# Expert weights of a two-layer mixture-of-experts model: which loads are requested while the tokens are still being routed

## The reference

```
def run_block(args):
    xb, e = args
    return (jax.nn.silu(xb @ w1[e]) * (xb @ w3[e])) @ w2[e]
...
p_sel, g_idx = lax.top_k(p_group, 1)
p_top, e_local = lax.top_k(jax.nn.softmax(e_logits, axis=-1), TOP_K)
e_idx = g_idx * EXPERTS_PER_GROUP + e_local
```

## Time and profile before

| | |
|---|---|
| median of 3 runs | 2667.68 us (2663.33, 2667.68, 2667.91) |
| profiled execution: its own time | 2663.74 us |
| its span (first to last instruction) | 2661.5 us |
| mean granted clock of TensorE | 0.906 of full speed |
| PE busy | 2262.7 us, 85% of the span |
| DVE, ACT, POOL busy | 731.6, 605.4, 174.1 us |
| moved by DMA | 595.85 MB, mean 224 GB/s |
| of it on SP's queue | 515.42 MB |
| routing of layer 0 ends, experts' block begins | at about 886.8 us |
| routing of layer 1 ends, experts' block begins | at about 2045.3 us |

### The profile page before, as it was taken

How to read it: one execution, slowest core, us unless ns; L and a number is a source line. 1 busy time by engine, 2 the same in 40 slices (tenths; PEclk the granted TensorE clock), 3 DMA queues, 4 the chain that set the end, 5 groups by cost and what they waited for, 6 DMA issues and landing times. The chain is left out here.

```text
span 2661.5 us, 34953 instructions
## 1 busy us (share of the span) xinstructions
PE 2262.7 (85%) x15232; PEld 1083.6 (41%) x15232; DVE 731.6 (27%) x1142; ACT 605.4 (23%) x915; POOL 174.1 (7%) x126
## 2 busy tenths in 40 slices
PE   6598998987995599999999639995985999988874
PEld 3277886554453133333333224442433333322223
DVE  0522324653006111111111273544225111111104
ACT  2521113551005111111111144445013111111102
POOL 0001000000000000000000212223000000000002
PEclk8599999997997799999999759997896999999986
DMA  9600105206422789889999430001005899999985
GB/s 376 224 24 21 35 24 211 113 1 189 158 95 74 320 325 415 355 350 411 416 414 414 138 114 24 24 0 58 6 3 243 335 411 417 414 416 419 427 342 194
DMA packets 139501, 595.85 MB, mean 224 GB/s; under 512 B 25333, under 2 KB 52689, under 8 KB 114641
## 3 DMA queue, kind: packets, MB, share of 16 engines
q1 hardware_dynamic: 109232, 515.42, 48.7%
q0 software_dynamic: 11952, 43.52, 4.5%
q10 hardware_dynamic: 18160, 34.61, 3.6%
HBM read 534.79 MB, written 58.72 MB: 223 GB/s over the span
## 5 line engine op out<-in xcount | busy, mean ns | idle before, releaser
L1584 PE MATMUL ph<-w,x_t 128*32 128x512 f32 x6016 | 683.2, 607 | 40.2 <-DMA w<-in_exp_w 38.0
L1584 PEld LDWEIGHTS ph<-w,x_t 128*32 128x32 f32 x6016 | 190.7, 112 | 455.2 <-issue 427.8
L1597 PE MATMUL py<-w,g_t 128*32 128x512 f32 x3008 | 341.2, 594 | 1.0 <-DVE g_t L1703 1.0
L1697 DVE TENSOR_TENSOR hidden<-hidden,ph 64x512 f32<-64x512 f32 x94 | 102.1, 1086 | 779.1 <-ACT hidden L1655 779.1
L1167 PE MATMUL z<-Y,w_o 128*128 128x512 f32 (+1 forms) x640 | 256.2, 557 | 0.0
L1655 ACT ACTIVATE hidden<-ph 64x512 f32<-64x512 f32 x94 | 55.6, 592 | 697.9 <-PE ph L1584 697.9
L1889 PE MATMUL z<-hT,w_cd 128*128 128x512 f32 (+1 forms) x448 | 185.7, 572 | 7.5 <-ACT hT L478 4.9
L1597 PEld LDWEIGHTS py<-w,g_t 128*32 128x32 f32 x3008 | 93.8, 110 | 204.9 <-issue 203.6
L692 PE MATMUL z<-h_high,w_hi 128*128 128x512 f32 (+1 forms) x432 | 161.7, 374 | 15.4 <-DVE h_low L526 15.4
L1167 PEld LDWEIGHTS z<-Y,w_o 128*128 128x128 f32 x640 | 120.7, 192 | 129.2 <-issue 125.9
L1562 POOL DMA_INDIRECT x_rows<-h_tokens,index x47 | 44.4, 945 | 1807.7 <-PE px L1569 995.2
(11 more groups left out here) (293 smaller groups left out, 2102.8 us busy)
## 6 DMA issues: line engine op xcount, KB each, us to landing
w<-in_exp_w SPq DMA_DIRECT2D x192, 2048.0 KB, 15.2
ada_raw<-in_ada_w SPq DMA_DIRECT2D x24, 2048.0 KB, 8.7
y_slots<-y_rows ACTq DMA_DIRECT2D x188, 128.0 KB, 8.7
y_slots<-zero SPq DMA_DIRECT2D x29, 512.0 KB
h_tokens<-h_rows ACTq DMA_DIRECT2D x18, 512.0 KB, 2.9
w_ab<-in_w_in_ab SPq DMA_DIRECT2D x14, 512.0 KB, 3.9
w_cd<-in_w_in_cd SPq DMA_DIRECT2D x12, 512.0 KB, 6.4
x_t_saved<-xT SPq DMA_DIRECT2D x8, 640.0 KB, 8.1
```

The source lines that it names most:

```text
L1584: ins = pe.matmul(ph[row:row + UNIT, :], xt[:, k, at:at + UNIT], w13[place[2 * b + n] % RING][:, half, k, :], start=(k == 0), stop=(k == K ...
L1597: ins = pe.matmul(py[b % 2][row:row + UNIT, :], gt[:, k, n * UNIT:(n + 1) * UNIT], w2[place[2 * b + n] % RING][:, k, half * 512:(half + 1) ...
L1697: dve.tensor_tensor(hid[PAIR:P, :].rearrange("s (k q) -> s q k", k=FT), hid[0:PAIR, :].rearrange("s (q k) -> s q k", k=FT), ph[PAIR:P, :]. ...
```

## The change

In `route`, SP now issues only the up and gate weights (w1 and w3) of expert 0. The loads of expert 0's w2 and of expert 1's w1 and w3 are taken out there. In `experts`, SP first waits for `s_x` to reach 16, which is the landing of the first gather of token rows. Behind it SP issues expert 0's w2, and then experts 1 and 2 in full. All other waits, buffers and the order of the loads among themselves stay.

```
@@ -1287,8 +1287,6 @@
                 sp.wait_ge(s_table, 1)
                 first = self.expert_of(sp, 0)
                 self.load_up(sp, layer, ring, 0, first)
-                self.load_down(sp, layer, ring, 0, first)
-                self.load_up(sp, layer, ring, 1, self.expert_of(sp, 1))
                 for i in range(HROWS):
                     sp.wait_ge(s_hw[i], 16 * len(range(i, nt, HROWS)))
 
@@ -1528,8 +1526,9 @@
 
             @block.sync
             def _(sp):
-                self.load_down(sp, layer, ring, 1, self.expert_of(sp, 1))
-                for j in range(2, NE):
+                sp.wait_ge(s_x, 16)
+                self.load_down(sp, layer, ring, 0, self.expert_of(sp, 0))
+                for j in range(1, NE):
                     e = self.expert_of(sp, j)
                     if j >= RING:
                         sp.wait_ge(s_a, last[j - RING] // 2 + 1)
```

## The result

| | before | changed |
|---|---|---|
| median | 2667.80 us (4 runs, 2663.33 to 2668.73) | 2646.31 us (4 runs, 2642.22 to 2651.92) |
| profiled execution, its own time | 2663.74 us | 2651.92 us |
| its span | 2661.5 us | 2649.4 us |

The ratio is 0.9924, with a 95% interval of 0.9901 to 0.9947: 20.3 us less, between 14.1 and 26.4. The two medians alone lie 21.5 us apart. The forecast was 2644.5 us. The profiled execution of the changed kernel is the slowest of its four, so I compare stages, each counted from its own start.

The account below looks back on a forecast made before the run. It took TensorE to bound layer 0's experts and the weights' stream layer 1's. Gains of 9.9 + 6.5 us in layer 0 and 6.5 in layer 1, 22.9 together, led to a 2644.5 us forecast, range 2636 to 2655.

Parts of the forecast that it names:

- The end of routing in layer 0: Layer 0's first gather starts earlier because the stores of rows land sooner with fewer loads beside them; gain 9.9 us.
- The landing of the gather: First gather of each layer lands in 4.5 us with no new loads beside it; gain 6.5 and 6.8 us.
- The weights behind the wait: Counted from the gather's landing L, block 3's weights land at L + 35.8, before up(3) needs them; 0 us lost.
- the bound of -1.5 us: Layer 0, up(3): at 396 GB/s the weights land at L + 38.1, 1.5 us late.
- the slack of 3.4 us: Layer 1, up(3): time left between the landing of the weights at L + 35.8 and their need at L + 39.2.
- Layer 1: Layer 1's experts: the weights' stream can gain 7.3 us and TensorE's start gains 6.8; 6.5 us taken.
- The gather's 11 us are its own: Rival, first gathers: the landing stays slow; layer 0 gains 9.9 us, layer 1 0.5 or less; about 2657.5 us; chance 0.08.
- The weights are just late: Rival, both layers: stream at 396 GB/s, and up 0's tail beside the gather; gain 16.4 us, 2651.3 us; chance 0.14.
- The clock: Rival, TensorE's first products: clock after idle time shifts either layer by up to 2.5 us; chance 0.10 for over 2 us.
- TensorE waits at block 3: Rival, up(3): below 275 GB/s, waiting for experts 1 and 2 eats layer 0's 16.4 us; 2684 us at 250; chance 0.02.
- The signs: Expected trace: layer 0's gather starts about 877, stores' wait about 12 us, block 3's wait under 2, layer 1's about 38.0.

Follow-up runs that it names:

- e5: The changed kernel with expert 0's w1 and w3 issued behind SP's wait for the stores of rows, in both layers; 2646.70 us, ratio 0.9926.
- e1: The changed kernel without its new wait: the loads taken out of routing are issued at the start of the experts' block; 2660.98 us, ratio 0.9986.
- e7_best: The changed kernel with expert 0's w1/w3 behind the stores' wait in layer 0 alone, and experts 1 and 2's w1/w3 before their w2; 2645.59 us, ratio 0.9924.
- e4_ups_first: The changed kernel with w1 and w3 of experts 1 and 2 issued ahead of their w2, behind expert 0's w2; 2645.75 us, ratio 0.9924.

## Why the prediction was right

**The forecast as a whole** held: 2646.31 us against 2644.5, inside 2636 to 2655. The sum was 22.9 us; by the stages it is 19.3. By the ratio of the runs it is 20.3 us, with an interval (14.1 to 26.4) wide enough for both. That the median came within 2 us of the forecast is in part luck: the four executions spread over 9.7 us, and the forecast of the stages was 3.6 us too high. These are its steps.

**The end of routing in layer 0** is the term that was mis-sized: 9.9 us forecast, 6.9 measured (T to gather 11.46 to 4.55). The mechanism was right, as e5 and e1 show: the stores hold up the meeting of the engines, and the loads beside them are what slows them. Wrong was the working. I let 5.76 MB pass at 396 to 426 GB/s, added 1 us for the last landing, and had the stores landed 11.8 us behind the last one's issue. It took 14.5. In these rows the first stretch begins where my sum began (861.0 us, here 1.84 later) and ends with the landing:

```profile
862.84:880.54 17.70, 4.67 (x176) 3.71 (x174) 11.54 (x32) 3.84 (x8) 0.00 (x0) 0.65 0.89 342
...
870.00:874.00 4.00, 0.16 (x12) 0.16 (x16) 3.79 (x8) 0.00 (x0) 0.00 (x0) 0.50 1.04 442
874.00:877.50 3.50, 2.61 (x161) 2.26 (x157) 1.20 (x7) 0.00 (x0) 0.00 (x0) 0.50 0.95 370
877.50:880.60 3.10, 0.00 (x0) 0.00 (x0) 0.00 (x0) 0.00 (x0) 0.00 (x0) 0.50 0.33 131
```

342 GB/s over 17.7 us are 6.05 MB and not 5.76: more than three stores were still under way. That is worth 0.7 us at the rates of my sum. The 1 us for the last landing stood on no row. From 878.5 us on only 0.01 MB still moved, and the last landing came at 880.5, 2.0 us later. The remaining 1.0 us is the rate, 386 GB/s on the mean until 878.5. The gather then starts 1.2 us behind the landing, where I had taken 0.9.

**The landing of the gather** was forecast at 4.5 us in both layers and is 4.47 and 4.51 (4.61 and 4.38 again): 6.6 and 6.8 us gained against 6.5 and 6.8. By the rule of the Trainium skill's "DMA: Bandwidth & Descriptors", section "Anatomy of one DMA — SWDGE (gpsimd) path", it would have been 3.2 us, an estimate; in all twelve profiles, with 47 gathers each, none lands in less than 4.2 us.

**The weights behind the wait.** SP issued down 0 0.72 us behind the landing in both layers (0.76 forecast). Up(3) of layer 0 needed expert 2 at L + 36.6 exactly as worked out, but it was there at L + 37.6 instead of L + 35.8, so the bound of -1.5 us was the better guess: 1.03 us lost. The rate of the bound is the one that came, 399 GB/s from 887 to 912.5 us where I had taken 426. In layer 1 the slack of 3.4 us covered it. In the second profile of the changed kernel the clock was lower (0.81 from up(0) to up(2), against 0.94 in the first), up(3) stood 36.70 us behind up(0), and there was no wait.

**Layer 1** gained 6.81 us by the stages (6.69 in the second pair), 6.5 forecast. The shift of the start came through to the end unshortened, though the weights' stream sets the end there. The reason given, that the stream's idle time shrinks by about as much as the start moves, agrees with what the DMA engines moved in the 312.95 us from the issue of up 0 on, before and then changed:

```profile
2031.14:2344.09 312.95, 286.94 (x2681) 94.67 (x2685) 47.26 (x84) 45.48 (x67) 13.27 (x14) 0.95 0.97 398
...
2025.62:2338.57 312.95, 290.39 (x2709) 96.00 (x2713) 48.22 (x85) 46.06 (x68) 13.23 (x14) 0.96 0.99 407
```

9 GB/s more over 313 us are 2.8 MB, or 6.6 us at 426 GB/s, and in the first 113 us alone (365 and 389 GB/s) it is already 6.4 us. I had 7.3 us for the stream and took 6.5. With the 2 to 3 us by which layer 1 differs between profiles anyway, an agreement to 0.3 us is more than the forecast can claim.

**The rivals.** *The gather's 11 us are its own*: fallen, by 4.5 us with nothing beside it and 11.8 in e1. *The weights are just late*: its first half happened at less than half of its price (1.03 us of 2.5, all of it in layer 0), its second half (the tail of up 0 beside the gather) did not, but e5 shows what it costs, 6.78 us. *The clock*: it moves the first products by what I said, but the two profiles compared hardly differ in it (36.33 against 36.06 us in layer 1; in layer 0 the difference is the wait). Up(0) to up(3) takes 33.4 to 34.5 us in some stages and 36.0 to 36.7 in others. The same changed kernel had 34.53 and 36.70 in layer 0, so the spread is that of executions. This rival is worth as much as the smaller terms of the sum. *TensorE waits at block 3*: the wait is there, 1.03 us and not 16. The engines moved 399 GB/s from 887 to 912.5 us and 425 behind it, far from 275.

**The signs.** The landing (4.5 us), down 0 (0.72 us), block 3 (under 2 us) and the waits of layer 1 (37.0 us from 2100 us on) were as said. SP's wait for the stores was not: 17.2 us, where I had about 12. So the first gather of layer 0 started at 881.7 and not at 877, of which 1.84 us are this profile's lateness.

## What to carry to other kernels

A small gather that starts a stage should not share the DMA engines with prefetches that nobody needs yet; here 0.52 MB took 4.5 us alone and 9 to 12 us beside 2.10 MB or more asked for at the same moment. Keep just the load that the first product needs in the earlier stage, as it fills the time until the gather: with more of it the gain goes, and with none of it too. When pricing such an edit, count every byte still under way and the time from the last bytes to the landing (2.0 us here), and compare stages from their own start, since single executions differed by 10 us in parts that no edit touched.

## What the runs showed that I had not expected

The landing of a 0.52 MB gather does not grow in step with the bytes beside it: 4.4 to 4.6 us beside nothing, 9.3 and 9.6 beside 2.10 MB, 12.0 and 11.7 beside 4.19 MB, 11.0 to 11.8 beside 8.4 MB. Beside 2.10 MB most of its bytes pass when the load is through. Beside 4.19 MB and more it gets through with its share before the load ends. In the crowded stretches further on other gathers took up to 13.7 us.

In layer 0 the last table ended anywhere from 873.3 us (e7_best) to 883.9 us (e4_ups_first). All of this spread lies ahead of the first edit: from the ranking's table (written at 857.35 to 867.96) to the end of the last one it is 15.90 to 15.92 us in all twelve profiles, whatever loads are issued there. The two profiles of one kernel differ by 0.8 and 1.7 us only, so how much of the spread of 10 us between one kernel's executions this is stays open.
